# One program of 36 weight stages on one Trainium2 core: no products of zeros at five turns

## What is computed

```python
def first_block(x, ...):              # 2 layers
    for i in range(2):
        mix = mlstm_mixer(x, ...) if i == 0 else mla_mixer(x, ...)
        x = layer_norm(DN_ALPHA * x + mix, ...)
        x = layer_norm(DN_ALPHA * x + peer_ffn(x, ...), ...)      # 16384 experts
        x = x + sigmoid(x @ ple_w_gate[i]) * (p[i] @ ple_w_proj[i])
def second_block(x, ...):             # 1 layer
    x = x + 0.5 * rms_norm(swiglu(rms_norm(x), w_in, w_out))      # ffn1
    x = x + rms_norm(token_mixing(rms_norm(x), ...))              # retention and attention
    x = x + 0.5 * rms_norm(swiglu(rms_norm(x), w_in, w_out))      # ffn2
```

## Time and profile before

| | |
|---|---|
| median of 3 runs | 2619.03 us (2618.84 to 2619.05) |
| profiled execution | 2619.5 us |
| its span | 2617.7 us |
| TensorE busy | 2579.7 us, 99% |
| VectorE, ScalarE, GpSimd busy | 1738.9, 1498.3, 669.4 us |
| mean granted clock of TensorE | 0.998 |
| HBM | 170 GB/s over the span |

### The profile page before, as it was taken

One profiled execution on the slowest core, in us unless ns is written; L12 is line 12 of the kernel. 1 busy time (PEld: TensorE's weight loads), 2 busy tenths in 40 slices (PEclk: granted clock), 3 DMA queues, 4 the chain that ended last, 5 costly groups with the idle time before them and its releaser, 6 DMA issues.

```text
span 2617.7 us, 43833 instructions
## 1 busy us (share of the span) xinstructions
PE 2579.7 (99%) x14973; PEld 2212.8 (85%) x14978; DVE 1738.9 (66%) x3203; ACT 1498.3 (57%) x2863; POOL 669.4 (26%) x310
## 2 busy tenths in 40 slices
PE   8999999999999999999999999999999999999998
PEld 7789998887888887799988887888888887877887
DVE  4568778886555565459778885555567746555774
ACT  4445588885455554454588884445556545564553
POOL 0007876772000000018877771000001000001000
PEclk9999999999999999999999999999999999999999
DMA  6255544445565554355544456666556665535564
GB/s 224 81 165 176 182 161 154 155 159 197 193 192 192 192 169 146 105 163 183 178 158 156 154 164 201 193 193 192 192 177 196 187 196 168 161 109 162 168 192 153
DMA packets 124331, 447.66 MB, mean 171 GB/s; under 512 B 14312, under 2 KB 14952, under 8 KB 123936
## 3 DMA queue, kind: packets, MB, share of 16 engines
q1 hardware_dynamic: 120096, 434.16, 51.8%
q0 software_dynamic: 2608, 9.08, 1.2%
q10 hardware_dynamic: 1488, 2.59, 0.3%
HBM read 444.74 MB, written 1.05 MB: 170 GB/s over the span
## 4 chain that ended last, share of the span: by engine, by line
PE 93%; DVE 2%; ACT 2%; DMA 1%; issue 1%; POOL 0%; ACTq 0%; DVEq 0%; POOLq 0%
PE ps L827 42%; PE ps L783 20%; PE ps L788 10%; PE ps L799 4%; PE ps L805 4%; PE ps L802 4%; PE ps L1046 3%; PE ps L1118 1%; PE ps L1015 1%; ACT w_hi L434 1%; PE ps L887 1%; PE ps L734 0%; PE ps L1064 0%; DMA ring<-in_v 0%; DMA ring<-in_ffn_in 0%
## 5 line engine op out<-in xcount | busy, mean ns | idle before, releaser
L434 ACT CAST w_hi<-ring 128x1024 fp32r<-128x1024 f32 (+1 forms) x812 | 852.1, 1050 | 761.7 <-PE ps L827 513.5
L446 DVE TENSOR_TENSOR w_lo<-ring,w_hi 128x1024 fp32r<-128x1024 f32 x545 | 664.7, 1220 | 553.6 <-ACT w_hi L434 544.4
L446 POOL TENSOR_TENSOR w_lo<-ring,w_hi 128x1024 fp32r<-128x1024 f32 x267 | 640.5, 2399 | 838.5 <-ACT w_hi L434 639.9
L827 PE MATMUL ps<-w_hi,x_parts 128*128 128x512 f32 x2976 | 745.4, 391 | 4.1 <-ACT w_hi L434 2.5
L827 PEld LDWEIGHTS ps<-w_hi,x_parts 128*128 128x128 f32 x2976 | 554.2, 188 | 125.7 <-issue 8.2
L783 PE MATMUL ps<-x_parts,w_hi 128*128 128x512 f32 x2320 | 592.0, 397 | 0.7 <-ACT w_hi L434 0.6
L783 PEld LDWEIGHTS ps<-x_parts,w_hi 128*128 128x128 f32 x2320 | 416.0, 189 | 76.3 <-ACT w_hi L434 1.1
L827 PE MATMUL ps<-w_lo,x_parts 128*128 128x512 f32 x1488 | 402.6, 389 | 0.4 <-DVE w_lo L446 0.3
L788 PEld LDWEIGHTS ps<-x_parts,w_lo 128*128 128x128 f32 x2320 | 316.5, 190 | 22.6
L827 PEld LDWEIGHTS ps<-w_lo,x_parts 128*128 128x128 f32 x1488 | 278.2, 188 | 59.5 <-DVE w_lo L446 1.7
L788 PE MATMUL ps<-x_parts,w_lo 128*128 128x256 f32 x2320 | 323.0, 282 | 0.0
(11 more groups left out here) (287 smaller groups left out, 2280.0 us busy)
## 6 DMA issues: line engine op xcount, KB each, us to landing
ring<-in_u SPq DMA_DIRECT2D x256, 512.0 KB, 3.5
ring<-in_v SPq DMA_DIRECT2D x256, 512.0 KB, 4.3
ring<-in_ffn_in SPq DMA_DIRECT2D x88, 512.0 KB, 4.0
ring<-in_ffn_out SPq DMA_DIRECT2D x44, 512.0 KB, 4.2
ring<-in_wq SPq DMA_DIRECT2D x32, 512.0 KB, 3.5
ring<-in_ple_gate SPq DMA_DIRECT2D x16, 512.0 KB, 4.3
SC<-in_rows POOLq DMA_DIRECT2D x11, 512.0 KB, 5.0
ring<-in_a_qk SPq DMA_DIRECT2D x8, 512.0 KB, 4.5
```

What stands on the lines that cost most here:

```text
L434: nc.scalar.copy(part(w_hi, i)[:, used(name)], tile(i)[:, used(name)]).then_inc(tiles_hi, 1)
L446: eng.tensor_tensor(part(w_lo, i)[:, at], tile(i)[:, at], part(w_hi, i)[:, at], ALU.subtract).then_inc(tiles_low[LOW[n][0]], 1)
L827: mm = nc.tensor.matmul(acc[:, 2 * tb + f, 0:cnt], x[:, k + c, tb * P:(tb + 1) * P], part(w, i)[:, at:at + cnt], start=(first and n == 0 a ...
```

## The change

The numbers of zero products at ml_out (24), the latents (8), rms1 (24), rms2 (26) and rms3 (26) become 0. The entry ml_out is left out of the table, and with it, at ml_out, one wait for a slot that the turn's loop makes anyway. Nothing else is different; the results are the same, as the products of zeros were overwritten.

```diff
--- before.py
+++ after.py
@@ -72,7 +72,7 @@
 RET_H = 4
 
 
-FILLERS = {"latents": 8, "ml_out": 24, "ln0_0": 0, "ln0_1": 0, "ln1_0": 0, "ln1_1": 0, "rms1": 24, "rms2": 26, "rms3": 26}
+FILLERS = {"latents": 0, "ln0_0": 0, "ln0_1": 0, "ln1_0": 0, "ln1_1": 0, "rms1": 0, "rms2": 0, "rms3": 0}
 RET_SCALE = 128 ** -0.5
 NA_SCALE = 64 ** -0.5
 FF_TILES = 2816 // P
```

## The result

| | before | after |
|---|---|---|
| median | 2619.12 us (20 runs, 2616.33 to 2621.73) | 2623.53 us (20 runs, 2622.04 to 2625.57) |
| ratio to before | | 1.0017, 95% interval 1.0011 to 1.0023 |
| profiled execution, its span | 2619.5 us, 2617.7 us | 2623.1 us, 2621.2 us |
| TensorE busy | 2579.7 us | 2563.0 us |
| mean granted clock | 0.998 | 0.993 |

The interval is +2.9 to +6.0 us. All of it lies above zero, so the change does cost something. It lies on both sides of the prediction's 0.2% (5.2 us), with the median under it.

What follows compares the result with a forecast made beforehand. TensorE, busy for 99% of the span, was taken to bound the kernel. The terms 3 x 1.9 - 0.6 + 0 + 0 = +5.1 us gave a forecast of 2624.1 us, range 2621.0 to 2630.0.

Steps and rivals of the forecast that it cites:

- The zeros hide under waits: At all five places the zeros lie under waits ended by another engine; removal alone gives 0, at most -0.1 us each.
- Three rms turns at 1.9 each: At rms1, rms2, rms3 the clock falls in the gap; 20 cold records delay ScalarE's first copy, +1.9 us each.
- lower bound of 1.3: Each rms turn: if the clock returned after 3 us, 15 records would be cold and the term 1.3 us.
- -0.6 after rms1: After rms1, a later TensorE shortens its 0.57 us wait for a late high part: -0.6 us, bounds -0.6 to 0.
- ml_out 0: At ml_out the clock is low before and after, and VectorE releases the second half: 0, bounds -1.9 to +0.8 us.
- The latents 0: At the latents the 2.3 us idle stretch brings no clock fall: 0; up to +2.7 us if it falls.
- the rival: The latents' turn falls to the low clock too: +2.7 us more, 2626.8 us in all; chance 0.15.
- The chances: Slower by over 0.2% (5.2 us, line at 2624.3 us) 0.52, within 0.46, faster 0.02.
- the turn's products don't bring the clock back: TensorE stays low through each rms turn and 5.5 us behind: 2.7 us more each, 2632.2 us; chance 0.10.
- not slower: Clock holds through the 5.2 to 5.9 us gaps, or is back before ScalarE is late: 0; chance 0.13.

Runs made afterwards that it cites:

- overlong: 36 zero products instead of 26 at rms2 and rms3, against the kernel before: 2621.69 us against 2618.24, ratio 1.0011.
- rms1_none: No zero products at rms1 alone (24 become 0), against the kernel before: 2620.50 us against 2618.91, ratio 1.0006.
- rms23_none: No zero products at rms2 and rms3 alone (26 each become 0), against the kernel before: 2621.41 us against 2618.91, ratio 1.0012.
- half_early: 13 zero products instead of 26 at rms2 and rms3, at the idle stretch's start, against the kernel before: 2621.63 us against 2618.24, ratio 1.0012.
- late_few: 7 zero products at rms2 and rms3, after a wait for VectorE's first half of x, against the kernel before: 2620.86 us against 2618.86, ratio 1.0007.
- ml_latents_none: No zero products at ml_out (24) and the latents (8) alone, against the kernel before: 2619.58 us against 2618.91, ratio 1.0002.
- more_zeros: Zeros against before: ml_out 37 plus 5 between its turn's halves, latents 10, rms2 and rms3 27: 2616.73 us against 2618.91, ratio 0.9992.
- start_too: The added zeros of more_zeros, plus 24 ahead of TensorE's first wait for input, against the kernel before: 2616.91 us against 2618.86, ratio 0.9993.
- the parts' own runs: rms1_none, rms23_none and ml_latents_none, each against the kernel before: ratios 1.0006, 1.0012 and 1.0002.
- transposes_x4: No zeros at ml_out, and the eight transposes of its turn's second half made four times (32); a single execution, no time drawn from it.
- half_late: 13 zero products at rms2 and rms3, after a wait for VectorE's first half of x, against the kernel before: 2621.68 us against 2618.24, ratio 1.0013.
- ml_more_only: Only ml_out gets more zeros, 37 and 5 between its turn's halves, against the kernel before: 2616.93 us against 2618.86, ratio 0.9991.

## Why the prediction was right

Forecast 2624.1 us, measured 2623.53; +5.1 us against +4.4, by the steps:

- **The zeros hide under waits: right.** The releasers didn't come sooner, and overlong showed the price, 1.7 us for 2.1 us of zeros too many, as soon as the cover is gone.
- **Three rms turns at 1.9 each: right in mechanism and size.** After has 1.69, 2.11 and 2.07. Over all the turns that ran low from their start (nine with rms1_none, rms23_none, half_early and late_few), it was 1.35 to 2.14. The spread goes with the time at which the clock came back, which was wider than the 4.2 to 5.5 us assumed: where it was back 2.9 to 3.0 us into the turn the cost was 1.35 to 1.42 (three turns), at 3.6 us 1.69, at 4.4 to 6.0 us 2.07 to 2.14 (five turns). For the early return the prediction had the lower bound of 1.3.
- **-0.6 after rms1: fits, not settled.** The wait is gone, 0.73 us, in both traces whose rms1 turn was late (after, rms1_none). With the turn on time it stands in 8 of 11 traces, 0.4 to 0.8 us, and is missing in 3 (ml_latents_none, more_zeros, start_too). So it varies by itself, and that the late turn removed it was argued, not shown.
- **ml_out 0: right for the turn, probably wrong for a_out.** Turn to stage is 3.95 us with and without its zeros. But the prediction took the low stretch in a_out for given, with -1.9 as a bound if the clock were back before it. In all three traces without the zeros it was back before or just as a_out began, which is worth 1.2 us against the mean of the seven with 24.
- **The latents 0: wrong.** The clock fell in both traces without their zeros, after 2.4 us of idleness. I had put the place nearer to the 1.2 us gap; the price, +2.7 in the rival, was too high as well. It is 0.97 and 1.24 us: the turn's 20 records took 1.3 us longer and not 1.9 (4.10 and 4.04 us against 2.75), the clock was back by the time of the up projections, for which I had charged 0.8, and in after 0.3 us of wait ahead of them went away.
- **The sum** by what the terms measured: 1.69 + 2.11 + 2.07 - 0.73 + 0.97 = +6.1 in one pair of traces; the parts' own runs give +4.8 (1.6 + 2.5 + 0.7), the change's 20 runs +4.4 with an interval of 2.9 to 6.0. The 6.1 is a little over the interval's end; with the 1.2 us that a_out gains it is +4.9. The forecast's nearness is thus in part luck: it missed about 1 us of cost at the latents and, as the traces have it, about as much gain in a_out, and the two cancel.
- **The chances.** 0.52 stood on slower by over 0.2%, 0.46 on within; the median is within, by 0.8 us.
- The rival "the turn's products don't bring the clock back" fell by transposes_x4 and by every rms turn; "not slower" by the five low stretches.

## What to carry to other kernels

Dummy products that fill TensorE's wait are worth half of the time for which the clock would be low behind it, but only where TensorE is what the next step waits for; behind a turn that VectorE holds up (ml_out's second half) they gave nothing until they reached to the end of both waits, and 24 of them seem worse than none, since in most traces they put the low stretch off into the next stage. Count them to the end of the wait, within some tenths of a us: half the number bought nothing (half_early), and 2.1 us of zeros more than before, 1.8 of them beyond the wait, cost 1.7 (overlong). Don't put them at the end of the idle stretch, where the clock has fallen or falls on them: 13 took 4.65 us instead of 2.98 (half_late), 7 took 3.15 instead of 1.67 (late_few).

## What was not expected

- Executions of one kernel differ by some us: 2616.3 to 2621.7 for before in 20 runs. ml_more_only, whose profiled execution never leaves the full clock between its start and its end, has 2615.5 to 2617.6 in 11. Of the 87 executions of before beside the experiments, the 7 with a mean clock of 0.999 have medians of 2615.9, 2617.4 and 2616.2 us in the three sets, the 73 with 0.998 have 2619.0, 2618.2 and 2619.1, but the 7 with 0.997 have 2618.4 to 2618.8, so the clock isn't all of it. A part of the spread comes from when the clock falls and returns, shown in before at a_out (low until 123.9) and in rms23_none, which has the same zeros there and was at the full clock from 119 on.
- 3.0 us of idleness brought the clock down at one turn and not at the other in the same execution (late_few).
- At the start the clock column shows 1.00 though the products ran low: a gate product lasts 634 ns (median) in before and 379 in start_too. There the durations decide.
